# An encoder layer with routed experts: the copies of the experts' output rows, from two engines to one

## The reference

```python
for e in range(N_EXPERTS):                       # 16
    a, u = jnp.split(t @ w_ei[e], 2, axis=-1)    # 1024 -> 2 x 512
    y = y + gate[:, e:e + 1] * ((jax.nn.silu(a) * u) @ w_eo[e])   # 512 -> 1024
```

## Time and profile before

| | us |
|---|---|
| median of 3 runs | 1485.11 |
| lowest and highest | 1481.98, 1485.95 |
| the profiled execution, its own time | 1487.16 |
| its span, first to last instruction | 1485.5 |
| experts, from the first one's matmuls to the last one's output | about 978 to 1435 |

### The profile page before, as it was taken

One profiled execution on the slowest core, in us unless ns is written; L12 is line 12 of the kernel. 1 busy time (PEld: TensorE's weight loads), 2 busy tenths in 40 slices (PEclk: granted clock), 3 DMA queues, 4 the chain that ended last, 5 costly groups with the idle time before them and its releaser, 6 DMA issues.

```text
span 1485.5 us, 20119 instructions
## 1 busy us (share of the span) xinstructions
PE 1328.4 (89%) x7662; PEld 1126.2 (76%) x7663; DVE 755.8 (51%) x980; ACT 627.5 (42%) x764; POOL 282.1 (19%) x286
## 2 busy tenths in 40 slices
PE   3999999999988999999999999377999999899960
PEld 1888878888888988877888889356788778778850
DVE  1333256421475333255422464667955766885546
ACT  1332354432222332354432231556845564874434
POOL 0332000000110142000000110125433432652310
PEclk9999999999999999999999999679999999999985
DMA  7954500024693444400024642499977977996416
GB/s 145 271 116 95 100 5 1 1 57 95 160 217 109 89 96 86 100 15 1 1 57 84 172 103 97 154 329 303 314 247 223 339 239 251 319 355 222 139 39 241
DMA packets 161232, 222.42 MB, mean 150 GB/s; under 512 B 20391, under 2 KB 135975, under 8 KB 160359
## 3 DMA queue, kind: packets, MB, share of 16 engines
q1 hardware_dynamic: 137296, 177.40, 42.9%
q0 software_dynamic: 12192, 34.51, 8.3%
q10 hardware_dynamic: 11676, 9.54, 2.1%
HBM read 200.19 MB, written 34.32 MB: 158 GB/s over the span
## 4 chain that ended last, share of the span: by engine, by line
PE 73%; DMA 7%; DVE 6%; issue 6%; ACT 4%; ACTq 2%; POOL 1%; SPq 1%; POOLq 0%; DVEq 0%
PE banks L638 18%; PE banks L640 18%; PE banks L639 18%; PE banks L832 4%; DMA moe_raw<-in_w_expert_in 3%; PE banks L799 2%; PE banks L771 2%; PE banks L836 2%; DMA raw<-in_w_in 2%; ACTq L1023 2%; PE banks L916 1%; DVE moe_lo L1631 1%; ACT moe_hi L1195 1%; PE banks L782 1%; PE banks L838 1%
## 5 line engine op out<-in xcount | busy, mean ns | idle before, releaser
L1631 DVE TENSOR_TENSOR moe_lo<-moe_raw,moe_hi 128x2048 fp32r<-128x2048 f32 x102 | 232.9, 2288 | 72.1 <-ACT moe_hi L1195 71.8
L1195 ACT ACTIVATE moe_hi<-moe_raw 128x2048 fp32r<-128x2048 f32 x102 | 195.1, 1914 | 53.6 <-PE banks L640 39.7
L1331 DVE TENSOR_TENSOR wlo<-raw,whi 128x2048 fp32r<-128x2048 f32 (+1 forms) x52 | 116.0, 2230 | 181.3 <-ACT whi L1046 181.3
L638 PE MATMUL banks<-xT,whi 128*128 128x512 f32 x448 | 174.9, 390 | 0.6 <-DVE wlo L1331 0.6
L640 PE MATMUL banks<-xT,wlo 128*128 128x512 f32 x448 | 174.4, 389 | 0.0
L639 PE MATMUL banks<-xT,whi 128*128 128x512 f32 x448 | 174.4, 389 | 0.0
L638 PE MATMUL banks<-moe_lo,xeh 128*128 128x512 f32 x368 | 147.4, 401 | 10.2 <-issue 4.9
L638 PE MATMUL banks<-wlo,xT 128*128 128x256 f32 x512 | 148.2, 289 | 7.4 <-DVE xT L1447 7.4
L639 PE MATMUL banks<-whi,xT 128*128 128x256 f32 x512 | 146.0, 285 | 0.0
L640 PE MATMUL banks<-whi,xT 128*128 128x256 f32 x512 | 145.8, 285 | 0.0
L640 PE MATMUL banks<-moe_hi,xel 128*128 128x512 f32 x368 | 145.3, 395 | 0.0
(11 more groups left out here) (247 smaller groups left out, 2475.2 us busy)
## 6 DMA issues: line engine op xcount, KB each, us to landing
moe_raw<-in_w_expert_in SPq DMA_DIRECT2D x128, 512.0 KB, 5.5
raw<-in_w_in SPq DMA_DIRECT2D x80, 512.0 KB, 6.8
moe_raw<-in_w_expert_out SPq DMA_DIRECT2D x64, 512.0 KB, 7.4
raw<-in_w_out SPq DMA_DIRECT2D x16, 512.0 KB, 6.8
toeplitz_rows<-bias_rows POOLq DMA_DIRECT2D x4, 1152.0 KB, 13.2
kqv<-in_x SPq DMA_DIRECT2D x8, 512.0 KB, 10.4
pt<-in_x SPq DMA_DIRECT2D x2, 2048.0 KB, 9.6
raw<-in_w_branch_a SPq DMA_DIRECT2D x8, 512.0 KB, 5.9
```

The costliest lines, as they stand in the source:

```text
L638: mm(dst, left[0], right[1], start=first, stop=False)
L1195: A(moe_hi[m % SPLIT_E], moe_raw[m % RAW_E], ACT.Copy).then_inc(e_hi, 1)
L1331: V.tensor_tensor(view(lo, shape), view(raw[c % 2], shape), view(hi, shape).bitcast(F32), ALU.subtract).then_inc(w_split, 1)
L1631: V.tensor_tensor(moe_lo[m % SPLIT_E], moe_raw[m % RAW_E], moe_hi[m % SPLIT_E].bitcast(F32), ALU.subtract).then_inc(e_lo, 1)
```

## The change

ACT makes all four copies of an expert's output rows, and DVE makes none. PE's wait before it writes bank 4 or 6 again is now on ACT's counter alone, once for each half.

```diff
@@ gpsimd
-                        pool.wait_ge(y_act, z * 2 + 3)
-                        pool.wait_ge(y_dve, z * 2 + 3)
+                        pool.wait_ge(y_act, z * 4 + 7)
@@ tensor, turn_acts
                     pe.wait_ge(h_done, z * HALVES + half + 3)
-                    if half == 0:
-                        pe.wait_ge(y_act, z * 2 + 1)
-                        pe.wait_ge(y_dve, z * 2 + 1)
+                    pe.wait_ge(y_act, z * 4 + 1 + 2 * half)
@@ scalar
-                        for d in range(2):
-                            A(y_sb[b][:, d * 512:(d + 1) * 512], bank[4 + d][:, :], ACT.Copy, scale=slot_gate(b, 0)).then_inc(y_act, 1)
+                        for d in range(4):
+                            A(y_sb[b][:, d * 512:(d + 1) * 512], bank[4 + d][:, :], ACT.Copy, scale=slot_gate(b, d // 2)).then_inc(y_act, 1)
                         e_split(pair, b * ECH + XCH + 1 + SPLIT_E)
@@ vector, before the loop
-            for sm, k in (..., (h_turned, 2), (y_act, 1), (y_dve, 1)):
+            for sm, k in (..., (h_turned, 2), (y_act, 3)):
@@ vector, in the loop
                         e_split(pair, b * ECH + 4 + SPLIT_E)
-                        dve.wait_ge(e_used, SPLIT_E + z * ECH + ECH)
-                        dve.wait_ge(y_gone, z + 1)
-                        dve.wait_ge(scatter_ids_in[b], pair * 16 + 16)
-                        for d in range(2):
-                            V.tensor_scalar(y_sb[b][:, D + d * 512:D + (d + 1) * 512], bank[6 + d][:, :], slot_gate(b, 1), None,
-                                            ALU.mult).then_inc(y_dve, 1)
                         e_split(pair, b * ECH + XCH + 1 + SPLIT_E)
```

More of the change, by code:

```diff
@@ L371, in encoder_kernel @@
         silu_done, h_done, h_turned, h_hi, h_lo = [sem(n) for n in ("silu_done", "h_done", "h_turned", "h_hi", "h_lo")]
-        y_act, y_dve = sem("y_act"), sem("y_dve")
+        y_act = sem("y_act")
         y_out = [sem(f"y_out{i}") for i in range(2)]
@@ L1511, in _ @@
             used = 16
-            for sm, k in ((e_used, SPLIT_E), (e_lo, RAW_E), (rows_T, 8), (xe_lo, 2), (h_done, 2), (h_turned, 2), (y_act, 1), (y_dve, 1)):
+            for sm, k in ((e_used, SPLIT_E), (e_lo, RAW_E), (rows_T, 8), (xe_lo, 2), (h_done, 2), (h_turned, 2), (y_act, 3)):
                 for _i in range(k):
```

## The result

| | before | after |
|---|---|---|
| median of 15 runs, us | 1484.55 | 1492.10 |
| lowest and highest | 1481.93, 1490.93 | 1488.25, 1500.77 |
| profiled execution, own time | 1487.16 | 1495.56 |
| its span | 1485.5 | 1493.9 |

The ratio is 1.005, with a 95% interval of 1.0038 to 1.0063: the change makes the kernel 0.5% slower. The forecast was 1493.7 us (0.58% more) and slower.

What follows compares the result with a forecast made beforehand. PE, busy 89% of the span, was taken as the bound, waiting in the experts' stage for h_full. Terms 4.6 + 2.2 + 1.0 + 0.3 + 0.5 = 8.6 us took the median 1485.11 to 1493.7 us; range 1488.0 to 1500.0.

Steps and rivals of the forecast that it cites:

- The chain and its price: Full-to-small expert seams: ACT's copies lead without a gap to PE, so two more copies make PE 1.15 us later.
- four seams with a table load: Expert seams 5 to 6, 7 to 8, 9 to 10, 11 to 12: 1.15 us later each, 4.6 us.
- two seams without: Small-expert seams 2 to 3 and 10 to 11, no table load: low part and h_full 1.1 us later each, 2.2 us.
- end: After the last expert: ACT's last copy ends later, and the final sum and layer norm follow, 1.0 us.
- PE's waits: At turn_acts the h_done wait moves to a register instruction ahead of the transpose: 0.3 us, bounds nothing and 1.1.
- clock: Four waits grow to 2.3 to 2.4 us and may lower PE's clock: 0.5 us, bounds 0 and 6.6.
- The seams at nothing: Seams 0 to 1, 1 to 2 and nine into full experts: slack covers the added copies, no cost.
- rival of four falls that nothing takes back: Clock falls at all four table-load seams, nothing recovers it: 14.7 us more, 1499.8 us; chance 0.13.
- Small: A later load or overlooked slack absorbs the shift at the table-load seams: 3.2 us more, 1488.3 us; chance 0.15.
- Faster: DVE's own work sets the pace in small experts, so relief gains at most 11.6 us, some 1479 at half; chance 0.06.
- What would show it: Signs expected in the changed profile: ACT's copy time, DVE's and PE's waits, h_full total about 25 us, full experts' length.
- signs of being wrong: Small experts keeping their lengths, or their second wait shrinking by what the first grew, would refute the prediction.

Runs made afterwards that it cites:

- e3: Kernel before, with two extra ACT copies into free tiles ahead of its own two, DVE keeping its copies; 1490.33 us, ratio 1.0052.
- e4: Kernel before, with DVE's two copies left out (group 1's rows stay zero) and ACT's two kept; 1483.14 us, ratio 0.9994.
- e6: Kernel before, with all four copies of odd experts on DVE and even experts still two and two; 1481.54 us, ratio 0.9986.
- e10: Kernel before, with an added, always met PE wait on ACT's counter, so the h_done wait sits ahead of the transpose; 1485.06 us, ratio 1.0010.
- e2: Changed kernel with PE's two waits in the other order, which puts the h_done wait back on the transpose; 1489.91 us, ratio 1.0041 of the kernel before.
- e8: Kernel before, with three copies on ACT and one on DVE, h_done wait on the transpose; 1485.21 us, ratio 1.0009.
- e11: Kernel before, with even experts' four copies on ACT and odd experts' four on DVE; 1485.45 us, ratio 1.0010.
- e5: Kernel before, with all four copies on DVE and none on ACT; 1485.21 us, ratio 1.0003.
- e9: e4 with POOL also waiting for DVE's low part of split 5 before it starts the sums; 1486.28 us, ratio 1.0020 of the kernel before.

## Why the prediction was right, step by step

**The chain and its price: right.** The prediction went from ACT's copies through split 5, the table load, split 0, the low part and `h_full` to PE. The timeline shows each link 1.15 to 1.16 us late. e3 shows the loss with ACT's load alone, e4 none with DVE's relief alone, and e6 a gain in experts 6, 8 and 10, where the same link is shortened.

| term | forecast, us | measured in experts 3 to 15 and at the end |
|---|---|---|
| four seams with a table load | 4.6 | first waits +1.23, +1.23, +1.23, +1.07 = 4.76 |
| two seams without | 2.2 | experts 3 and 11: 1.32 + 1.29 = 2.61 |
| end | 1.0 | 0.8 (POOL's last operation +1.0) |
| PE's waits | 0.3 | 0.70 in full experts; the rest is in the two rows above |
| clock | 0.5 | 1.9: 4.4 of slower work, less 2.5 of shorter second waits (0.2 of it without a fall, in expert 8) |
| waits for `hT` and `xel` | nothing | -1.3 (experts 6, 8 and 12) |
| sum | 8.6 | 9.5 |

Experts 6, 8, 10 and 12 grew by 5.35 us. Their first waits grew by 4.76, their second waits shrank by 2.5, the waits for `hT` and `xel` shrank by 1.3, and PE's time outside all of these grew by 4.4 (1.7, 0.1, 1.3 and 1.3). So the sum came out partly by luck: the clock cost 1.2 us more than forecast, and 1.3 us that the sum didn't have came off. From the last matmul to POOL's operation 2.7 us pass, 1.7 before. The 9.5 us are one execution's against one. The medians differ by 7.55 us, and the interval of the ratio is 5.6 to 9.4 us, which holds the forecast's 8.6.

**The seams at nothing: right.** In experts 1 and 2 the `h_full` waits are 1.54 and 1.54 us, 1.48 and 1.47 before. Full experts have no wait of a copy's size. The prediction counts nine seams into full experts; with seven full experts there are seven. That changes nothing in the sum.

For SP's loads the prediction said that at the seams that slip, everything slips with them, and took nothing. That isn't quite what came: the late loads that experts 6 and 8 already had took up part of the shift (ACT's wait for chunk 3 in expert 6 went from 1.97 to 0.56 us). Expert 8 shows it best, since no clock fell there: its first wait grew by 1.23 us and the expert by 0.93.

**PE's waits: a term that was too small.** I counted "the 18 transposes in small experts" and took 0.3 us "since the wait itself is the same". e10 gives 1.07 us for this alone. The full experts should have been counted too: the transpose's idle time goes from 0.12 to 0.20 us in each, although `h_full` is there long before PE comes. That fits the order of instructions (the waits now sit on two instructions in a row ahead of the transpose), and e2, which puts `h_done` back on the transpose, goes back to 0.12. What inside PE takes this time no run shows.

**The clock: too small a term.** The granted clock fell to 0.50 for 3.41 us in experts 6, 10 and 12, three of the four seams; in the kernel before it stayed at 1.00 from 1033 us to the end of the experts. I had let a fall cost up to 1.65 us, of which the second wait takes back most, and 0.5 us for all. PE's own work took 1.7, 1.3 and 1.3 us longer in the three experts. Their second waits gave back 0.99, 0.34 and 1.28 us, so 1.7 us stay; the other 0.2 of the row are expert 8's, which had no fall. The path, falls that the second wait partly takes back, was the one said; that it would be three of four and less given back wasn't. Expert 8 had the same wait of 2.48 us and no fall. e2 and e3, with waits of 2.40 and 2.59, fell at two of four seams, e8, with 1.83, at one, and e10, with waits of up to 1.5 us there, at none. In e11 no fall followed even the 2.99 us in expert 11. So in these runs the length of the wait doesn't decide it. The rival of four falls that nothing takes back (14.7 us) didn't come, since one seam had no fall and the second waits gave back 2.5 us.

**The other rivals.** *Small* needed a load or slack to absorb the shift; the first waits for `h_full` grew by the full amount. Its idea was not empty: in experts 6 and 8 loads were late in the kernel before and absorbed part of the shift, as said, and in e4, e6 and e11 ACT waits for a load in experts 3 or 11. *Faster* hung on whether DVE, freed, finds its next high part ready. It does not: 5.38 and 2.33 us of wait, and e4's ratio of 0.9994. The Trainium skill's rule that offloading from a saturated DVE may make sense ("Perfetto Trace Analysis", section "Optimizing Scalar/DVE Operations") is not borne out here, since DVE was full by its sum, 19.47 us of 20.66, yet one engine behind in the chain. e5 and e6 show that the reverse move shortens the small experts behind full ones.

**What would show it.** ACT's four copies to the next high part: 2.30 us, as said. DVE's wait at the full seam: over 4, as said. First waits of 2.3 to 2.4: 2.48, and 2.23 in expert 12; the excess is the place of the wait. New waits of about 1.1 in experts 3 and 11: 1.18 and 1.19. Total for `h_full` about 25: 24.7, though 1.4 us of it are the seven waits in full experts, which the list of before leaves out at 0.12 us each, and shorter second waits offset that. Full experts would keep 35.65: wrong by 0.08. One of its two signs of being wrong came true in part: the second wait shrank by 0.99 us in expert 6 and by 1.28 in expert 12, where the first had grown by 1.23 and 1.07. Yet these experts grew by 1.50 and 0.70 us, because the slower clock used the time; in expert 8, without a fall, the second wait stayed.

## What to carry to other kernels

When work can go to either of two engines, the sums of busy time don't decide it: follow the wait that ends last back through the seam, and load the engine that waits there for the other. The answer can differ from one seam to the next in the same loop; here DVE has room for all four copies behind full experts, where ACT also loads a table, and none at the seams between small ones, 2 to 3, 10 to 11 and 11 to 12 (e5, e6). When a wait is added ahead of an instruction of PE, look at where the older wait comes to sit, since a wait off the instruction itself cost 0.08 us at each pass of a full expert, where it was met.

## What the runs showed of the hardware

- **A tiny operation of POOL waits for DVE's subtraction.** L592 adds 128x1 elements. It lasts 0.19 us alone, and 2.16 us here, when DVE is in a `moe_lo` at the time. At the end of e6 POOL's (first fence) and DVE's operation (second) end within 0.1 us of each other:

```profile
1428.25 2.16 POOL L592 TENSOR_TENSOR wait_bearer<-wait_bearer 128x1 f32<-128x1 f32 x1 [26.58 <-DVE y_sb L1684]
```

```profile
1428.08 2.28 DVE L1632 TENSOR_TENSOR moe_lo<-moe_raw,moe_hi 128x2048 fp32r<-128x2048 f32 x1
```

In e6 POOL's operation begins 3.0 us after the last matmul instead of 1.7, and lasts 1.97 us longer; 2.0 of these 3.3 us reach the end. The change itself frees POOL from most of these collisions. Minimum, median and maximum of its durations in ns, in the kernel before (first) and after (second):

```profile
L592 POOL TENSOR_TENSOR wait_bearer<-wait_bearer x48: 187/1364/2432, 975.9 to 1436.2; 128x1 f32<-128x1 f32 x48
```

```profile
L592 POOL TENSOR_TENSOR wait_bearer<-wait_bearer x48: 187/194/2802, 971.6 to 1444.7; 128x1 f32<-128x1 f32 x48
```

The Trainium skill, "SBUF — State Buffer", section "Who interferes with whom", says that a DVE instruction with two inputs in SBUF contends with a GpSimd instruction that reads SBUF, and that the contention is an exclusive lock. These rows agree with it: both operations end within 0.1 us.

- **Transfers that start earlier can cost.** With the sums' DMAs 3.5 us earlier in the expert (e4), ACT waited 1.85 us for a load of weights, and with them held back (e9) the wait was gone. With them 2.4 us earlier (the changed kernel, where ACT is later as well) there was none.

- **A wait that is met isn't free on PE.** At a full expert's transpose PE's idle time is 0.20 us when the wait for `h_done` sits on an instruction ahead of it (e10, the changed kernel), and 0.12 us when it sits on the transpose (e2, the kernel before).

- **Waits of the same length did and didn't bring the clock down.** After waits of 2.40 to 2.59 us in experts 6, 8 and 10 it fell to 0.50 in some places and stayed at 1.00 in others of the same execution, and it fell once after 1.83 us (e8).
